# Attention's softmax division moved behind the values: transposed unscaled, row sums spread by small products, the branch added by GpSimd

## The reference

```python
h = rms_norm(x, norm_mix[l])
x_rec, x_gate, c_q, c_kv, k_rot, g_rec, g_att = split(h @ w_in[l])
rec_out = gelu(x_gate) * h_rec                     # recurrent branch
s = einsum('bqhd,bkhd->bhqk', q, k) * QK_DIM ** -0.5
p = softmax(where(visible, s, -inf), axis=-1)      # 16 heads, chunk-causal
o = einsum('bhqk,bkhd->bqhd', p, v)
x = x + (sigmoid(g_rec) * rec_out + sigmoid(g_att) * o) @ w_out[l]
```

## Time and profile before

| | |
|---|---|
| median of 3 runs | 3554.67 us (3548.87 to 3555.1) |
| profiled execution | 3555.15 us, span 3553.4 us |
| TensorE, products | 3033.6 us, 85% of the span |
| VectorE | 1633.9 us, 46% |
| ScalarE | 982.0 us, 28% |
| GpSimd | 327.2 us, 9% |
| granted TensorE clock | 0.888 of full |

### The profile page before, as it was taken

One profiled execution on the slowest core, in us unless ns is written; L12 is line 12 of the kernel. 1 busy time (PEld: TensorE's weight loads), 2 busy tenths in 40 slices (PEclk: granted clock), 3 DMA queues, 4 the chain that ended last, 5 costly groups with the idle time before them and its releaser, 6 DMA issues.

```text
span 3553.4 us, 46204 instructions
## 1 busy us (share of the span) xinstructions
PE 3033.6 (85%) x17332; PEld 2522.5 (71%) x17332; DVE 1633.9 (46%) x3308; ACT 982.0 (28%) x1680; POOL 327.2 (9%) x459
## 2 busy tenths in 40 slices
PE   3888688888789999998889687888888699999996
PEld 2888577678788999997888576768888444444442
DVE  4666566665554433346675566665553200000001
ACT  1333244443333222122433244443332000000000
POOL 3000122220000000000000222220000100000001
PEclk9999788778888999998999777878888699999998
DMA  4212100002222222222122000002221589989985
GB/s 152 84 59 75 30 8 16 8 0 85 72 82 71 72 72 84 73 73 75 59 61 69 23 16 8 8 0 97 95 77 31 219 296 318 318 313 317 317 313 180
DMA packets 219142, 384.43 MB, mean 108 GB/s; under 512 B 34534, under 2 KB 156454, under 8 KB 218992
## 3 DMA queue, kind: packets, MB, share of 16 engines
q1 hardware_dynamic: 202640, 329.80, 28.1%
q0 software_dynamic: 16352, 52.67, 4.2%
HBM read 352.99 MB, written 29.44 MB: 108 GB/s over the span
## 4 chain that ended last, share of the span: by engine, by line
PE 69%; DVE 15%; issue 7%; ACT 6%; POOL 1%; DMA 1%; DVEq 0%; ACTq 0%; POOLq 0%
PE ACC L361 15%; PE ACC L363 14%; PE ACC L362 14%; PE ACC L765 12%; PE TP L765 6%; DVE TR L1384 2%; PE TP L515 1%; PE TP L361 1%; PE TP L786 1%; DVE nwt L1209 1%; PE TP L523 1%; PE ACC L530 1%; PE TP L362 1%; PE TP L363 1%; PE TP L535 1%
## 5 line engine op out<-in xcount | busy, mean ns | idle before, releaser
L361 PE MATMUL ACC<-XH,WH 128*128 128x288 f32 x1984 | 594.8, 300 | 46.1 <-DVE XP L1252 37.0
L363 PE MATMUL ACC<-XH,WL 128*128 128x288 f32 x1984 | 595.2, 300 | 0.0
L362 PE MATMUL ACC<-XL,WH 128*128 128x288 f32 x1984 | 595.2, 300 | 0.0
L765 PE MATMUL ACC<-MW,XT 128*128 128x512 f32 x1024 | 445.2, 595 | 1.1 <-ACT XT L1129 1.1
L361 PEld LDWEIGHTS ACC<-XH,WH 128*128 128x128 f32 x1984 | 380.1, 192 | 49.9 <-DVE XP L1252 38.5
L821 ACT ACTIVATE WH<-RAW 128x2048 fp32r<-128x2048 f32 (+1 forms) x129 | 238.1, 1845 | 539.3 <-PE ACC L363 534.8
L362 PEld LDWEIGHTS ACC<-XL,WH 128*128 128x128 f32 x1984 | 379.6, 191 | 0.0
L363 PEld LDWEIGHTS ACC<-XH,WL 128*128 128x128 f32 x1984 | 378.4, 191 | 0.0
L765 PEld LDWEIGHTS ACC<-MW,XT 128*128 128x128 f32 x1024 | 194.6, 191 | 240.6 <-issue 239.0
L1173 DVE TENSOR_TENSOR WL<-RAW,WH 128x2048 fp32r<-128x2048 f32 (+1 forms) x129 | 284.3, 2204 | 107.7 <-ACT WH L821 106.6
L1792 DVE SCALAR_TENSOR_TENSOR HT<-HT,ACC 128x1024 f32<-128x1024 f32 x16 | 19.5, 1222 | 657.3 <-ACT HT L1135 657.3
(11 more groups left out here) (454 smaller groups left out, 5864.0 us busy)
## 6 DMA issues: line engine op xcount, KB each, us to landing
MW<-in_moe_w_dram SPq DMA_DIRECT2D x192, 1024.0 KB, 5.4
RAW<-in_w_in_dram SPq DMA_DIRECT2D x36, 1024.0 KB
RAW<-in_ffn_w_dram SPq DMA_DIRECT2D x30, 1024.0 KB
dispatched<-ZT POOLq DMA_DIRECT2D x4, 2048.0 KB, 17.7
RAW<-in_w_out_dram SPq DMA_DIRECT2D x8, 1024.0 KB
RAW<-in_w_mk_dram SPq DMA_DIRECT2D x8, 1024.0 KB
RAW<-in_w_mv_dram SPq DMA_DIRECT2D x8, 1024.0 KB
RAW<-in_w_mq_dram SPq DMA_DIRECT2D x8, 1024.0 KB
```

Of the source, the lines that this page charges most:

```text
L361: nc.tensor.matmul(out, a[0], b[0], start=first, stop=False)
L362: nc.tensor.matmul(out, a[0], b[1], start=False, stop=False)
L363: return nc.tensor.matmul(out, a[1], b[0], start=False, stop=last)
L765: mm = nc.tensor.matmul(out[:, h, :], lhs[:, 2 * pair + j, :], MW[n % RING][:, j, h * 512:(h + 1) * 512], start=(pair, j) == (0, 0), stop= ...
```

## The change

The probabilities are no longer scaled. TensorE turns the bare exponentials, as soon as ScalarE has given the bank back (`exp01`, `exp23` are the counts at which it has). VectorE's `row_sums` takes the reciprocals of a head's row sums into columns of `sm`. Once a pair, TensorE's `row_scales` spreads them over the 64 output partitions of each head: ten products, each of a column of reciprocals (as weights, repeated 64 times) with the identity. VectorE multiplies `AO` by the result (`rows_scaled`). The gate (1 + TGA) is applied as the values leave PSUM (`head_output`). The addition of `REC` and the low part of the result go to GpSimd (`gated_sum` there), and `mixed_high` moves to the end of ScalarE's `attend(0)`. The factor 0.25 goes into the recurrent branch.

```diff
@@ TensorE
+                def row_scales():
+                    t.skip("r_inv", 1)
+                    pe.wait_ge(s["r_inv"], t.next("r_inv").n)
+                    banks = open_tp(), open_tp()
+                    for bank, tiles in zip(banks, ((0, 1, 2, 3), (4,))):
+                        for k, tt in enumerate(tiles):
+                            n = rows(tt)
+                            for h in range(2):
+                                mm = nc.tensor.matmul(bank[h * 64:h * 64 + 64, k * P:k * P + n],
+                                                      sm[0:n, 32 + 8 * h + tt:33 + 8 * h + tt].to_broadcast([n, 64]),
+                                                      ident[0:n, 0:n], start=True, stop=True)
+                        mm.then_inc(s["tp_ready"], 1)
@@ attend
                         weighted_values(1 - head)
+                        if head == 0:
+                            row_scales()
...
-                    pe.wait_ge(s["p01"], t.next("p01").n)
+                    pe.wait_ge(s["acc_free"], exp01)
                     turn_probabilities([P01[0], P01[1][:, 0:P], P01[1][:, P:2 * P]])
...
-                    pe.wait_ge(s["p23"], t.next("p23").n)
+                    pe.wait_ge(s["acc_free"], exp23)
...
                 weighted_values(1)
-                pe.wait_ge(s["mixed"], 8 * (layer + 1))
+                row_scales()
+                pe.wait_ge(s["mixed"], 8 * (layer + 1) + 1)
@@ ScalarE
-                    ins_.then_inc(s["p_exp"], 1)
+                    ins_.then_inc(s["acc_free"], 1)
...
-                    if tile is not None:
-                        mixed_high(tile)
                     if head == 0 and not last:
                         keys_out()
                     turned(lambda b: [(PTH[:, 2:9:3, :], b[:, 0:3 * P].rearrange("p (a b) -> p a b", a=3))])
                     turned(lambda b: [(PTH[:, 3:13:3, :], b.rearrange("p (a b) -> p a b", a=4))])
+                    if tile is not None:
+                        mixed_high(tile)
@@ VectorE
-                def head_output(head):
+                def head_output(head, tile):
                     mine = slice(head * 64, head * 64 + 64)
+                    if head == 0:
+                        dve.wait_ge(s["mixed"], t.next("mixed").n)
+                    gate = TGA[mine, bass.ds(tile, 1), :].rearrange("p o t -> p (o t)")
                     bank, m = take_tp()
-                    v.tensor_copy(AO[mine, 0:SEQ], bank[mine, :]).then_inc(s["tp_free"], 1)
+                    v.scalar_tensor_tensor(out=AO[mine, 0:SEQ], in0=gate[:, 0:SEQ], scalar=1.0, in1=bank[mine, :], op0=ALU.add, op1=ALU.mult)\
+                        .then_inc(s["tp_free"], 1)
...
+                def rows_scaled(m):
+                    dve.wait_ge(s["tp_free"], m.at(4))
+                    for cols in (slice(0, SEQ), slice(SEQ, T)):
+                        bank, m = take_tp()
+                        ins_ = v.scalar_tensor_tensor(out=AO[:, cols], in0=AO[:, cols], scalar=0.5, in1=bank[:, 0:cols.stop - cols.start],
+                                                      op0=ALU.mult, op1=ALU.mult).then_inc(s["tp_free"], 1)
+                    dve.wait_ge(s["tp_free"], m.at(4))
+                    marker("ao").then_inc(s["ao"], 1)
+                def row_sums(head):
+                    step(v.tensor_tensor(sm[0:NEW, 20:21], sm[0:NEW, 20:21], sm[0:NEW, 21:22], ALU.add))
+                    v.reciprocal(sm[:, 32 + 8 * head:32 + 8 * head + TT], sm[:, 16:16 + TT]).then_inc(s["r_inv"], 1)
@@ attend
-                    for k in range(2):
-                        v.tensor_scalar(P01[k], P01[k], sm[:, 32 + k:33 + k], None, ALU.mult)
-                    v.tensor_scalar(P0[:], P0[:], sm[0:NEW, 36:37], None, ALU.mult).then_inc(s["p01"], 1)
                     if not first:
-                        m = head_output(1 - head)
+                        m = head_output(1 - head, tile)
+                        if head == 0:
+                            rows_scaled(m)
...
-                    v.tensor_scalar(P23[0][:], P23[0][:], sm[:, 34:35], None, ALU.mult)
-                    v.tensor_scalar(P23[1][:], P23[1][:], sm[:, 35:36], None, ALU.mult).then_inc(s["p23"], 1)
...
+                    dve.wait_ge(s["acc_free"], m23.at(2))
+                    row_sums(head)
                     if following:
                         query_scales()
@@ GpSimd
+                def gated_sum(tile):
+                    ao = AO[:].rearrange("p (a b) -> p a b", a=1)
+                    tile = bass.ds(tile, 1)
+                    pool.wait_ge(s["ao"], t.next("ao").n)
+                    tt_(ao, ao, REC[:, tile, :], ALU.add).then_inc(s["mix_sum"], 1)
+                    pool.wait_ge(s["mix_hi"], t.next("mix_hi").n)
+                    tt_(YL[:, tile, :], ao, YH[:, tile, :].bitcast(F32), ALU.subtract).then_inc(s["mixed"], 1)
...
                     values_low()
+                    gated_sum(i)
                     assemble_keys()
```

More of the change, by code:

```diff
@@ L563, in attend @@
                     bank = open_acc()
+                    exp01 = t.last("acc", 2)
                     prompt_scores(bank, 0, 0)
@@ L569, in attend @@
                     bank = open_acc()
+                    exp23 = t.last("acc", 2)
                     prompt_scores(bank, 0, 2)
@@ L994, in attend @@
                     if not first:
-                        t.skip("tp", 2)
+                        t.skip("tp", 4 if head == 0 else 2)
                     if head == 0:
@@ L1034, in _ @@
                 split_high()
-                t.skip("tp", 2)
+                t.skip("tp", 4)
                 t.skip("v_lo", 1)
@@ L1504, in head_output @@
                     bank, m = take_tp()
-                    v.tensor_copy(AO[mine, SEQ:T], bank[mine, 0:NEW]).then_inc(s["tp_free"], 1)
+                    v.scalar_tensor_tensor(out=AO[mine, SEQ:T], in0=gate[:, SEQ:T], scalar=1.0, in1=bank[mine, 0:NEW], op0=ALU.add, op1=ALU.mult)\
+                        .then_inc(s["tp_free"], 1)
                     return m
-                def gated_sum(tile, m):
+                def rows_scaled(m):
                     dve.wait_ge(s["tp_free"], m.at(4))
-                    tile = bass.ds(tile, 1)
-                    ao = AO[:].rearrange("p (a b) -> p a b", a=1)
-                    step(v.scalar_tensor_tensor(out=ao, in0=TGA[:, tile, :], scalar=1.0, in1=ao, op0=ALU.add, op1=ALU.mult))
-                    v.scalar_tensor_tensor(out=ao, in0=ao, scalar=2.0, in1=REC[:, tile, :], op0=ALU.mult, op1=ALU.add)\
-                        .then_inc(s["mix_sum"], 1)
@@ L1517, in mixed_low @@
-                def mixed_low(tile):
-                    tile = bass.ds(tile, 1)
-                    dve.wait_ge(s["mix_hi"], t.next("mix_hi").n)
-                    v.scalar_tensor_tensor(out=YL[:, tile, :], in0=AO[:].rearrange("p (a b) -> p a b", a=1), scalar=0.25,
-                                           in1=YH[:, tile, :].bitcast(F32), op0=ALU.mult, op1=ALU.subtract).then_inc(s["mixed"], 1)
+                    for cols in (slice(0, SEQ), slice(SEQ, T)):
+                        bank, m = take_tp()
+                        ins_ = v.scalar_tensor_tensor(out=AO[:, cols], in0=AO[:, cols], scalar=0.5, in1=bank[:, 0:cols.stop - cols.start],
+                                                      op0=ALU.mult, op1=ALU.mult).then_inc(s["tp_free"], 1)
@@ L1557, in attend @@
                         queries_low()
-                    if tile is not None:
-                        gated_sum(tile, m)
                     turned(lambda b: [(PTL[:, 0, :], b[:, 0:P], PTH[:, 0, :]),
@@ L1565, in attend @@
                                       (PSL[:, 1:TT, :], b[:, NEW:TT * NEW].rearrange("p (a b) -> p a b", a=4), PSH[:, 1:TT, :])])
-                    if tile is not None:
-                        mixed_low(tile)
                     if head == 0 and not last:
@@ L1588, in _ @@
                     for pair in range(2):
-                        attend(1)
+                        attend(1, tile=i * 2 + pair)
                         attend(0, tile=i * 2 + pair)
-                attend(1, split=0)
+                attend(1, tile=6, split=0)
                 attend(0, tile=6, last=True)
-                attend(1, last=True)
+                attend(1, tile=7, last=True)
                 split_low()
-                gated_sum(7, head_output(1))
-                mixed_low(7)
+                rows_scaled(head_output(1, 7))
                 w_region_free()
@@ L1811, in _ @@
             load = pool.dma_start
-            for name, n in (("acc_free", 2), ("tp_free", 4), ("w_lo", 2), ("mem_place", 1)):
+            for name, n in (("acc_free", 2), ("tp_free", 4), ("w_lo", 2), ("mem_place", 1), ("mixed", 1)):
                 pool.sem_inc(s[name], n)
```

29 lines of the change are left out of this document (13 added, 16 removed).

## The result

| | before | after |
|---|---|---|
| median | 3554.59 us (3548.87 to 3555.1, 4 runs) | 3599.89 us (3591.53 to 3608.53, 4 runs) |
| span | 3553.4 us | 3599.7 us |
| TensorE busy | 3033.6 us | 3068.4 us |
| VectorE busy | 1633.9 us | 1544.2 us |
| granted TensorE clock | 0.888 | 0.885 |

The ratio is 1.0129, with a 95% interval of 1.0109 to 1.015: slower by 45 us. VectorE has 90 us less to do, and the kernel is slower, because VectorE was not what ended last where its work was taken away.

What follows compares the result with a forecast made beforehand. TensorE was taken to bound the kernel, with head 0's part a series of TensorE, ScalarE and VectorE. Terms summed to +25.0 us a layer, +50 us over two, giving 3604 us; range 3545 to 3632.

Steps and rivals of the forecast that it cites:

- case A: The whole program as summed from the terms: 3604 us, own range 3585 to 3632, chance 0.5.
- the lock: Head 0's query scales: GpSimd's subtraction and VectorE's small SBUF instructions exclude each other whole, +1.9 us a pair.
- the wait before `queries`: Sign of being right: TensorE's wait before head 0's `queries` grows from 2.25 to about 4 us.
- Handoff and scalings in head 1's part: Head 1's part: ScalarE's last exponential frees the bank itself, -0.45 us; VectorE's scalings go, -0.80 us of path.
- `row_sums`: In front of `query_scales` in both heads: an add, a wait and a reciprocal on the path, +0.37 us each.
- `row_scales`: TensorE after head 1's values, in head 0's part: twenty uncovered product instructions, 2.4 us, bounds 1.2 and 4.8.
- rival B: Output halves of `row_scales` run side by side (1.2 us), GpSimd hits scales little (+0.5): 3568 us, chance 0.2.
- Fair sharing: Alternative rule for GpSimd beside VectorE's query scales in head 0's part: about +0.7 us instead of +1.9.
- The other edits at nothing: Gate factors and 0.25, 0.5 in other places: same widths, same kind, 0 us.
- The end of a layer: After head 15's values, products, scalings, GpSimd and `YH` in series: 7.3 us, +3.6; last head 1 gives -1.0.
- C: Whole program, nothing measurable: 3548 to 3562 us, chance 0.1.
- D: Faster, as VectorE's load makes TensorE's waits and the clock need not fall: 3502 us, chance 0.2.

Runs made afterwards that it cites:

- b2: Changed kernel with the branch sum and YL subtraction back on VectorE and `mixed_high` ahead of `keys_out` again: 3582.71 us, ratio 1.0080 to the kernel before.
- a4: Changed kernel with both heads' `row_scales` products sent to the same output half, output not the reference's: 3604.16 us in one run.
- b1: Kernel before with GpSimd adding the branch and making YL, `mixed_high` behind PTH, probabilities still scaled: 3587.16 us, ratio 1.0091.
- a2: Changed kernel with `row_sums` taken before the low parts of keys and queries: 3595.55 us, ratio 1.0124 to the kernel before.
- c2: Changed kernel with YL subtraction behind the key sums, row sums early, `row_scales` behind `keys_and_values`: 3549.49 us, ratio 0.9974 to the kernel before.
- c3: c2 with the products and scalings of each layer's last head 0 back at the change's place: 3540.86 us, ratio 0.9958 to the kernel before.

## Why the prediction was right, and where its sizes were off

The forecast was 3604 us; it is 3599.89. The mechanism of case A held, the lock above all, but that the number is so close is luck: errors in its terms cancelled. Of the prediction's own signs three came as said (the wait before `queries` at 4.56 us, the stretched instructions, head 1's part shorter by 1.37). The twenty products at 2 to 2.6 us did not: with 1.35 they are nearer to the 1.2 that it had named as a sign of being wrong. By its steps:

1. *Handoff and scalings in head 1's part* (-0.45 and -0.80). In the pair shown, `queries` starts 4.35 us after the row maxima, where it was 4.55: -0.20. The small negative maxima in between took 0.46 us instead of 0.22 and ate the rest. From `queries` to L1271 (L1252 before) it is 629.48 to 634.88, 5.40 us, instead of 6.21: -0.81. The second number is right, the first too large.

2. *`row_sums`* (+0.37). From L1271 to `KTL`: 8.10 instead of 7.77, +0.33. Right in head 1's part; in head 0's it is less, 0.20 (b2). What goes beyond head 1's -0.88 is that the scores ran partly at the higher clock (the first of them 0.33 us at 644.45 instead of 0.47): -0.35 from there to the maxima. Together -0.20 - 0.81 + 0.33 - 0.08 - 0.35 = -1.11 for this pair, and -1.37 on average.

3. *`row_scales`* (+2.4 each). **The term that was mis-sized: 1.3.** The working priced twenty instructions one after the other from the earlier trace rows, rows in which all products go to the whole width. It named the side-by-side case as the lower bound and gave it to rival B because no row showed it. The Trainium skill (TensorEngine Tiling, "Key Properties") had it right that tiles of the array run in parallel; a4 against the changed kernel shows it now, 2.33 against 1.35 us.

4. *The lock* (+1.9). **Right in mechanism and place, a little low.** From the first `PTL` to the maxima +2.50, of which `row_sums` is 0.29 (619.56 to 619.85): +2.2. The subtraction fell on the scales at the moment laid out, and the first instruction that it held was one with a single input in SBUF (L1226, 1.26 us), which I had not counted among those that can be held. The rule of the Trainium skill (SBUF — State Buffer, "Who interferes with whom") agrees with these rows: whole instructions wait, and they end with GpSimd's. Fair sharing (+0.7) is out: in b1, where GpSimd's part of the change stands alone, the stretch grows by 2.28 us, and in b2, without it, by 0.20.

For the pair shown the sum closes: +1.3 for the products and +2.5 from `PTL` to the maxima are the +3.78 by which head 0's part grew (30.04 instead of 26.26). The mean of +4.39 is another sum: +3.4 without the clock's share, as the parts in which the loop turns grew by less than the others, and 0.95 for 2.2 us more at the lower level.

5. *The other edits at nothing.* Nothing speaks against it; they were not tried alone.

6. *The end of a layer* (+3.6 and -1.0). TensorE, layer 1:

```profile
2461.38 0.79 PE L361 MATMUL TP<-PTH,VH 128*128 128x512 f32 x1 [1.48 <-DVE PTL L1220]
...
2466.46 1.35 PE L564 MATMUL TP<-ident,sm 128*64 128x128 f32 x20
2472.61 0.60 PE L361 MATMUL ACC<-YH,WH 128*128 128x288 f32 x1 [4.79 <-POOL YL L1935]
```

From the products to the output projection 6.15 us, where the earlier trace rows has a wait of 3.72: +2.4, not +3.6, and the difference is the products' own. The -1.0 is not to be seen. From the last row maxima to the output projection it is 25.25 us instead of 19.69 in layer 1, and 28.02 instead of 19.82 in layer 0. Head 14's values, which began at 0.50 us a product before, began at 0.80 in both layers, and the clock stayed low behind them. In layer 0 it was so to the end, and there the twenty products themselves took 2.38 us. In all the two ends have 28.0 and 18.4 us at the lower level, where the kernel before has 9.6 and 9.5. By 0.43, which was measured in head 0's parts and is an estimate here, that is about 12 of the 13.8 us; with 2 x 2.4 for the series of products, scalings and GpSimd, it would leave room for the -1.0. a2, which differs from the changed kernel by the row sums alone, has the same two stretches in 18.5 us each, with 1.6 us at the lower level. Layer 1, changed kernel:

```profile
2452.00:2457.00 5.00, 5.00 (x24) 4.63 (x23) 0.89 (x2) 0.82 (x3) 0.00 (x0) 0.50 0.00 0
```

*The sum.* Twelve head 0 parts +52.7 us (predicted +56), fourteen head 1 parts -19.2 (-12.3), the first and last head 0 of each layer -0.7 (+1.2), two ends +13.8 (+5.2), the rest of the program -0.3: +46.3 us of span (+50). Without the clock's share the twelve head 0 parts would be +41 us, not +56. Products priced too high, and a gain in head 1 priced too low, were made up by the longer stretches at the lower clock, about 11 us in head 0's parts and about 12 at the ends. The sum had no term for them: the prediction had the clock only in rival D, as a gain, and in the upper end of its range.

*The rivals.* B had the price of the products right and the lock wrong, at +0.5; it forecast 3568. C falls with it. D needed head 1's part to be 4 us shorter; it was 1.37. Its other half, that a clock which need not fall is worth tens of microseconds, is borne out by size: 30 us lie between two executions of c2 (above). But the change did not earn it: its head 0 parts and its two ends have more time at the lower level, not less.

## What to carry to other kernels

Taking work off an engine pays only where that engine is the last to arrive: follow one turn of the loop and ask of each wait what released it before you count what the engine is rid of. When work goes to GpSimd, ask which small VectorE instructions on SBUF run beside it, since a chain of them is held for whole GpSimd instructions. And put added TensorE work where another engine is the last one: the same twenty products cost 1.3 us ahead of `keys_and_values` and next to nothing behind it, and c3 turned a loss of 1.3% into a gain of 0.4% by order alone. Before a difference is put down to an edit, compare like parts of the loop with like time at the lower clock; b2's time alone would have cleared GpSimd.

## What the runs showed of the hardware

- Plain float32 products with 64 columns of weights, sent in turn to the lower and the upper half of the output partitions, run side by side: twenty in 1.35 us, forty in 2.34; twenty into one half take 2.33. The same twenty take 2.39 and 2.38 us where the clock is at its lower level.
- GpSimd held a VectorE TENSOR_SCALAR of 128 by 5 numbers, SBUF to SBUF, for 1.26 us; it is 0.13 at home. The row maxima, which read PSUM, kept their times under a GpSimd subtraction of 1.41 us (c2: 0.41, 0.54 and 0.34 us, as in the kernel before).
- The time at TensorE's lower level in like parts of one loop goes from 2 to 12.8 us within a single execution, and a part's length grows by about 0.43 us for each of them. Between two kernels here this is worth some 20 us of the total (b2 against its sum), more than several of the terms argued over.
- Where VectorE's loop of three turns goes from one turn to the next, VectorE is idle for 2.97 to 3.26 us with no releaser in the profile, in every kernel here.
